# ScalarE instead of GpSimd makes the high halves of the weights in the index stage of a two-layer encoder

## The chip, the cores and the metric

The kernel runs on one core of one Trainium2 chip. The metric is the device time of one execution in microseconds (us). Engines are named as in the profile: PE is TensorE, ACT is ScalarE, DVE is VectorE, POOL is GpSimd, SP is SyncE; ACTq and SPq are the DMA issues of these engines.

## The reference

Two layers over 1024 tokens of width 1024. Layer 0 is attention of two kinds and a gated feed-forward. Layer 1 is sparse attention: an indexer scores all visible keys for each query, each query keeps its 256 best keys, and 16 heads attend to them. The change lies in the indexer:

```
h = x @ w_in
q, k_r, c_lat, q_idx, k_idx, w_idx = jnp.split(h, [c0, c1, c2, c3, c4], axis=-1)
q_idx = partial_rope(q_idx.reshape(b, s, IDX_HEADS, IDX_DIM), positions)   # 16 heads of 64
k_idx = partial_rope(k_idx, positions)
idx_logits = relu(einsum('bqhd,bsd->bhqs', q_idx, k_idx))
score = einsum('bqh,bqhs->bqs', w_idx, idx_logits) * IDX_SCALE
top_val, top_idx = lax.top_k(where(visible, score, -inf), 256)
```

All of it is float32. The kernel multiplies in bf16 by splitting every operand in two: a high half (the value rounded to bf16) and a low half (the value minus the high half, again bf16). A product is then three bf16 matmuls: high by high, high by low, low by high.

## The kernel before

Each engine has a program of its own, written out by hand, and runs it in that order; semaphores join them. Nothing reorders it.

**Weights.** SP loads strips of weights, 128 x 1024 float32 each, into four slots `w_stage[0..3]`. Each is split into `w_hi[slot]` and `w_lo[slot]`. SP may load a slot again when its low half is written (`w_split`). In the index stage of before both halves are made by POOL in `split_piece` (L266: multiply by one, write bf16; L269: subtract). Elsewhere a pair of helpers does it with two engines: `piece_hi` (L275) is an ACT copy, `piece_lo` (L282) the POOL subtraction.

**The index stage** follows the feed-forward of layer 0. Its sync, gpsimd, tensor, scalar and vector programs are `index_sync`, `index_gpsimd`, `index_tensor`, `index_scalar`, `index_vector`. Eight strips s = 0 to 7 of `l1_qidx` hold two index heads each, strip s in slot s % 4, so each slot is used twice (i = 0, then i = 1). While strip s is projected, POOL prepares the strip that comes four later: for s < 4 the second round of index strips, for s >= 4 the first four strips of `l1_q`, the query weights of the stage behind.

For each strip:

1. PE makes the projection in eight parts of six matmuls (L2012, `strip_unit`) into two PSUM banks. Between the parts it puts the score products of the strip two earlier (L2056, `scores(g)`).
2. ACT copies the strip to `strip_f` (L2084) and issues four DMAs (L2089) that bring it, with halves swapped, into `strip_w`. This is `copy_strip`.
3. DVE multiplies the PSUM copy by the cosine table (L2140). POOL multiplies `strip_w` by the sine table when the DMAs have landed (L2030, "the sine" below). DVE adds the two (L2146, "the rotation").
4. ACT rounds the rotated strip to bf16 (L2120, two instructions, `highs`), DVE makes the low half (L2178, `lows`).

**The scores.** A strip gives 12 score products, g = 12(s-2)+t with t = 0 to 11: two heads by six query blocks that see 384, 512, 640, 768, 896 and 1024 keys. For each, PE writes one of two PSUM bank pairs in turn (`bank = 2 * (g % 2)`), ACT applies ReLU into `positive[g % 4]` (L2112), and DVE multiplies by the head's weight and adds it to `score` (L2168, L2171, "the add"). PE waits before product g until ReLU g-2 is done (`pe.wait_ge(s_ir, g - 1)`), ACT before ReLU g until add g-4 is done.

ACT's order for one strip is `copy_strip`, ReLU t = 0 to 4, `highs`, ReLU t = 5 to 11, then the `copy_strip` of the next strip. DVE's is cosine, adds t = 0 to 2, rotation, adds t = 3 to 6, `lows`, adds t = 7 to 11. POOL's is the sine, then the split. Score products exist for ACT and DVE from s = 1 on.

At the stage's end PE waits for the last add (`pe.wait_ge(s_ia, IDX_STEPS * KT)`) before it goes on with the remaining query strips (L309), and DVE begins the search for the best 256 then.

Of the kernel before, what the change touches and what calls it, by code (L numbers as in the profile page):

```python
# [28 lines left out]
KT = D_MODEL // P  # L29
# [25 lines left out]
SLOTS = 4  # L55
# [48 lines left out]
def wait_if(eng, semaphore, value):  # L104

    if not isinstance(value, int) or value > 0:
        eng.wait_ge(semaphore, value)
# [39 lines left out]
def program(nc, t_in, out):  # L147
    with ExitStack() as ctx:
# [20 lines left out]
        def sem(name):  # L169
            return nc.alloc_semaphore(name)  # L170
# [30 lines left out]
        def banks(b):  # L201

            return ps[:, b:b + 2, :].rearrange("p a n -> p (a n)")


        w_loaded = [sem(f"w_loaded{s}") for s in range(SLOTS)]
        w_cast = [sem(f"w_cast{s}") for s in range(SLOTS)]
        w_split = [sem(f"w_split{s}") for s in range(SLOTS)]
        w_used = [sem(f"w_used{s}") for s in range(SLOTS)]
# [6 lines left out]
        def strips(name, per_body, iters):  # L216
            return Feed(uses, used, lambda n, i: t_in[name][per_body * i + n],
                        [(n, KT * P) for n in range(per_body)], iters)

        def row_tiles(name, tiles):  # L220

            return Feed(uses, used, lambda n, i: t_in[name][n % tiles],
                        [(n % SLOTS, D_MODEL) for n in range(2 * tiles)], 1)

        feed_o0 = row_tiles("l0_o", KT)
# [5 lines left out]
        feed_qidx = strips("l1_qidx", 4, 2)  # L231
        feed_q = strips("l1_q", 4, 8)
# [25 lines left out]
        def split_piece(pool, feed, n, i):  # L258
            slot, cols = feed.pieces[n]
            pool.wait_ge(w_loaded[slot], 16 * (feed.use(n, i) + 1))  # L260
            hi, lo = held(feed, n)
            if feed is feed_o0 and n >= SLOTS:
                pool.wait_ge(s_pj, 6 * N_PAIRS)
            else:
                pool.wait_ge(w_used[slot], feed.used(n, i))
            pool.tensor_tensor(hi, w_stage[slot][:, 0:cols], ones[:, 0:1].to_broadcast([P, cols]),  # L266
                               ALU.mult).then_inc(w_cast[slot], 1)
            pool.wait_ge(w_cast[slot], feed.use(n, i) + 1)
            pool.tensor_tensor(lo, w_stage[slot][:, 0:cols], hi, ALU.subtract).then_inc(w_split[slot], 1)  # L269

        def piece_hi(act, feed, n):
            slot, cols = feed.pieces[n]
            act.wait_ge(w_loaded[slot], 16 * (feed.use(n, 0) + 1))
            act.wait_ge(w_used[slot], feed.used(n, 0) - (feed is feed_o0 and n < KT + SLOTS))
            act.activation(w_hi[slot][:, 0:cols], w_stage[slot][:, 0:cols], ACT.Copy).then_inc(w_cast[slot], 1)  # L275

        def piece_lo(pool, feed, n):
            slot, cols = feed.pieces[n]
            pool.wait_ge(w_loaded[slot], 16 * (feed.use(n, 0) + 1))
            pool.wait_ge(w_used[slot], feed.used(n, 0) - (feed is feed_o0 and n < KT + SLOTS))  # L280
            pool.wait_ge(w_cast[slot], feed.use(n, 0) + 1)
            pool.tensor_tensor(w_lo[slot][:, 0:cols], w_stage[slot][:, 0:cols], w_hi[slot][:, 0:cols],  # L282
                               ALU.subtract).then_inc(w_split[slot], 1)

# [29 lines left out]
        def held(feed, n):  # L314

            if feed is feed_o0 and SLOTS <= n < KT:
                return xt_hi[:, n - SLOTS, :], xt_lo[:, n - SLOTS, :]
            slot, cols = feed.pieces[n]
            return w_hi[slot][:, 0:cols], w_lo[slot][:, 0:cols]
# [963 lines left out]
        def back_and_norm(tag, feed, tiles, act_hi, act_lo, names, free_at, bank_of, next_feed, early, load_x=None,  # L1283
# [161 lines left out]
            def scalar_program(act):  # L1445
# [18 lines left out]
                def piece_highs(first, last):  # L1464
                    if tiles == KT:
                        for n in range(first, last):
                            piece_hi(act, feed, n)
# [16 lines left out]
                if tiles == KT:  # L1484
                    piece_hi(act, next_feed, 0)
# [501 lines left out]
        def idx_step(g):  # L1987

            s, t = g // IDX_STEPS, g % IDX_STEPS
            return s, t // len(picky), picky[t % len(picky)], 2 * (g % 2)  # L1990

        def strip_bank(s):
            return 4 + 2 * (s % 2)
# [5 lines left out]
        def swaps_through(s):  # L1999


            return (64 if s % 2 == 0 else 32) + 64 * (s // 2 + 1)
# [24 lines left out]
        def index_gpsimd(pool):  # L2027
            def sine(w, tab, b, swapped):
                pool.wait_ge(s_sw5[b], swapped)
                pool.tensor_tensor(w, w, tab, ALU.mult).then_inc(s_s5, 1)  # L2030

            split_piece(pool, feed_qidx, 0, 0)
            pool.wait_ge(s_tl5, 64)
            sine(strip_w[0][:, :], rope_i[1][:, :], 0, 64)
            split_piece(pool, feed_qidx, 1, 0)
            sine(strip_w[1][0:ROPE, :], rope_q[1][:, :], 1, 32)
            split_piece(pool, feed_qidx, 2, 0)
            split_piece(pool, feed_qidx, 3, 0)
            for s in range(KT):
                sine(strip_w[s % 2][:, :], rope_i[1][:, :], s % 2, swaps_through(s))  # L2040
                if s < 4:
                    split_piece(pool, feed_qidx, s, 1)
                else:
                    split_piece(pool, feed_q, s - 4, 0)

        def index_tensor(pe):
            def scores(g):
# [31 lines left out]
        def index_scalar(act):  # L2079
            def copy_strip(m, bank, b, heads, used, swapped, rotated):  # L2080

                act.wait_ge(*used)
                wait_if(act, s_sw5[b], swapped)
                act.activation(strip_f[b][:, :], banks(bank), ACT.Copy).then_inc(s_f5, 1)  # L2084
                act.wait_ge(s_f5, m + 1)
                wait_if(act, s_a5, rotated)
                for a in range(0, 64 * heads, 32):
                    to = a + 32 if a % 64 == 0 else a - 32
                    act.dma_start(strip_w[b][to:to + 32, :], strip_f[b][a:a + 32, :]).then_inc(s_sw5[b], 16)  # L2089

            def small_used(n):
                return w_used[feed_small.slot(n)], feed_small.used(n, 0) + 1

            copy_strip(0, 0, 0, 2, small_used(0), 0, 0)
            copy_strip(1, 2, 1, 1, small_used(1), 0, 0)
            act.wait_ge(*small_used(2))
            act.activation(lat_hi[:, 1, :], banks(4), ACT.Copy).then_inc(s_h5, 1)
            act.wait_ge(*small_used(3))
            for h in range(2):
                src = ps[:, 6 + h, 0:4 * IDX_HEADS].rearrange("p (b n) -> p b n", b=4)  # L2100
                act.activation(w_idx[:, 4 * h:4 * h + 4, :], src, ACT.Copy, scale=IDX_SCALE).then_inc(s_w5, 1)
            act.wait_ge(s_a5, 1)
            act.activation(ki_hi[:, :], banks(0), ACT.Copy).then_inc(s_h5, 1)
            act.wait_ge(s_a5, 2)
            act.activation(lat_hi[:, 0, :], banks(2), ACT.Copy).then_inc(s_h5, 1)

            def relu(g):
                s, hh, i, bank = idx_step(g)
                act.wait_ge(s_iq, g + 1)
                if g >= 4:  # L2110
                    act.wait_ge(s_ia, g - 3)
                act.activation(positive[g % 4][:, 0:span[i]], banks(bank)[:, 0:span[i]], ACT.Relu).then_inc(s_ir, 1)  # L2112

            def highs(s):
                act.wait_ge(s_a5, 2 + s + 1)
                if s >= 2:
                    act.wait_ge(s_iq, IDX_STEPS * (s - 1))
                for hh in range(2):
                    rows = slice(hh * IDX_DIM, (hh + 1) * IDX_DIM)
                    act.activation(qi[s % 2][hh][rows, :], banks(strip_bank(s))[rows, :], ACT.Copy).then_inc(s_h5, 1)  # L2120

            for s in range(KT):
                copy_strip(2 + s, strip_bank(s), s % 2, 2,
                           (w_used[feed_qidx.slot(s % 4)], feed_qidx.used(s % 4, s // 4) + 1),
                           swaps_through(s) - 64, s + 1)
                for t in range(IDX_STEPS):
                    if s >= 1 and t < 5:
                        relu(IDX_STEPS * (s - 1) + t)
                    if t == 4:
                        highs(s)  # L2130
                    if s >= 1 and t >= 5:
                        relu(IDX_STEPS * (s - 1) + t)
            for t in range(IDX_STEPS):
                relu(IDX_STEPS * (KT - 1) + t)
# [612 lines left out]
```

## Time and profile before

| what | value |
|---|---|
| median of 3 runs | 2836.85 us (2831.59 to 2836.87) |
| profiled execution, its time | 2837.71 us |
| profiled execution, its span | 2835.9 us |
| PE busy | 2704.4 us (95%) |
| DVE busy | 1897.8 us (67%) |
| POOL busy | 1667.6 us (59%) |
| ACT busy | 1088.9 us (38%) |
| index stage, first strip to the first matmul behind it | 1286.98 to 1467.84 us of the span |

Busy time of PE includes the filling of its pipeline, so 95% is not a peak rate. The shares are means over the whole span; within the index stage they are others, and the engines there feed each other in a ring, so that a busy share alone does not say who sets the pace.

### The profile page before, as it was taken

The page shows a single profiled execution, that of the slowest core. Times are in us where ns is not written, and L with a number is a line of the kernel's source. Part 1 is how long each engine was busy: PE and PEld are TensorE (multiplying, and loading weights), DVE is VectorE, ACT ScalarE, POOL GpSimd, SP SyncE. Part 2 cuts the span into 40 slices and gives each one's busy share as a digit, 9 for nine tenths or more (in the row PEclk, how much of TensorE's full clock was granted, in tenths as well). Part 3 has the DMA queues.
Part 4 walks back from the last instruction along what each step waited for, and adds up shares of the span by engine and source line. Part 5 has one row for each costly group of instructions (what it writes and reads, how often), then busy time and mean ns, then how long its engine had stood idle before and what let it go on. Part 6 is the DMA issues. An engine that isn't in the chain of part 4 may idle for free.

```text
span 2835.9 us, 42627 instructions
## 1 busy us (share of the span) xinstructions
PE 2704.4 (95%) x16048; PEld 1358.3 (48%) x16048; DVE 1897.8 (67%) x2637; ACT 1088.9 (38%) x1665; POOL 1667.6 (59%) x916
## 2 busy tenths in 40 slices
PE   8999898899999999999899999889999999999998
PEld 4566554354444444444444444455554444444443
DVE  6787778576666674255999999777747756664043
ACT  3555556343333310014554343667743433331000
POOL 4676656336666779845347777711113566775884
PEclk9999999999999999999999999999999999999999
DMA  4222466631111253333213222588874211113332
GB/s 149 54 60 70 82 120 123 190 118 53 54 60 60 67 175 129 98 134 86 52 38 141 111 78 100 122 183 193 192 213 142 70 60 60 56 56 127 126 103 98
DMA packets 312621, 297.97 MB, mean 105 GB/s; under 512 B 252720, under 2 KB 252848, under 8 KB 312480
## 3 DMA queue, kind: packets, MB, share of 16 engines
q1 hardware_dynamic: 284832, 264.97, 32.4%
q10 hardware_dynamic: 27648, 31.07, 3.8%
q8 instruction: 94, 1.54, 0.2%
q14 instruction: 47, 0.39, 0.0%
HBM read 189.51 MB, written 35.70 MB: 79 GB/s over the span
## 4 chain that ended last, share of the span: by engine, by line
PE 79%; DVE 6%; DMA 5%; issue 4%; ACT 3%; POOL 2%; ACTq 1%; POOLq 0%; DVEq 0%; SPq 0%
PE ps L1684 23%; PE ps L327 20%; PE ps L309 14%; DMA pt<-split 5%; PE ps L643 4%; PE ps L2501 4%; PE ps L392 4%; PE ps L913 2%; PE ps L2012 2%; PE ps L2056 1%; PE ps L649 1%; DVE split L841 1%; PE ps L2518 1%; PE ps L884 1%; DVE prob L1037 1%
## 5 line engine op out<-in xcount | busy, mean ns | idle before, releaser
L266 POOL TENSOR_TENSOR w_hi<-w_stage,ones 128x1024 bf16<-128x1024 f32 (+1 forms) x115 | 238.3, 2072 | 137.7 <-PE ps L327 85.3
L269 POOL TENSOR_TENSOR w_lo<-w_stage,w_hi 128x1024 bf16<-128x1024 f32 (+1 forms) x115 | 266.0, 2313 | 9.0
L1501 DVE SCALAR_TENSOR_TENSOR x_res<-x_res,ps 128x1024 f32<-128x1024 f32 x32 | 39.0, 1218 | 319.7 <-PE ps L327 318.8
L327 PE MATMUL ps<-w_hi,hid_hi 128*128 128x512 bf16 x704 | 209.4, 379 | 0.8 <-POOL w_lo L269 0.8
L327 PE MATMUL ps<-w_hi,hid_lo 128*128 128x512 bf16 x704 | 209.4, 379 | 0.0
L327 PE MATMUL ps<-w_lo,hid_hi 128*128 128x512 bf16 x704 | 209.3, 379 | 0.0
L2501 PE MATMUL ps<-lat_hi,q_now 128*128 128x512 bf16 (+3 forms) x768 | 199.7, 330 | 6.7 <-DVE row_max L2566 6.7
L309 PE MATMUL ps<-xt_hi,w_hi 128*128 128x512 bf16 x608 | 181.5, 380 | 2.5 <-DVE score L2171 2.5
L309 PE MATMUL ps<-xt_hi,w_lo 128*128 128x512 bf16 x608 | 181.5, 380 | 0.0
L309 PE MATMUL ps<-xt_lo,w_hi 128*128 128x512 bf16 x608 | 181.3, 380 | 0.0
L1684 PE MATMUL ps<-xt_hi,w_hi 128*128 128x512 bf16 x432 | 163.7, 379 | 0.0
L1684 PE MATMUL ps<-xt_lo,w_hi 128*128 128x512 bf16 x432 | 163.7, 379 | 0.0
L1684 PE MATMUL ps<-xt_hi,w_lo 128*128 128x512 bf16 x432 | 163.7, 379 | 0.0
L1058 POOL TENSOR_TENSOR prob<-take,prob 128x1024 f32<-128x1024 f32 (+3 forms) x64 | 107.1, 1679 | 88.5 <-DVE prob L1037 70.5
L282 POOL TENSOR_TENSOR w_lo<-w_stage,w_hi 128x1024 bf16<-128x1024 f32 x28 | 66.1, 2367 | 149.4 <-ACT w_hi L275 149.4
L1449 ACT ACTIVATE ln_rstd<-ln_rstd 128x1 f32<-128x1 f32 x32 | 6.3, 202 | 374.6 <-DVE ln_rstd L1513 374.2
L2407 DVE MATCH_REPLACE8 score<-best,score 128x512 f32<-128x512 f32 (+4 forms) x160 | 148.8, 942 | 0.0
L1650 POOL TENSOR_TENSOR w_lo<-w_stage,w_hi 128x1024 bf16<-128x1024 f32 x36 | 76.9, 2136 | 113.6 <-ACT w_hi L1758 113.6
L2404 DVE MAX8 best<-score 128x8 f32<-128x512 f32 (+4 forms) x160 | 140.5, 944 | 1.8
L2624 POOL COPY v_now_hi<-val_hi 128x512 bf16 (+1 forms) x16 | 10.6, 661 | 217.9 <-PE ps L2518 217.8
L2566 DVE CUSTOM_DVE_ANT_0 prob<-ps,hide 128x1024 f32<-128x1024 f32 (+7 forms) x128 | 96.2, 751 | 59.9 <-PE ps L2501 59.8
L2550 ACT ACTIVATE prob<-prob,neg_max 128x1024 f32<-128x1024 f32 (+7 forms) x128 | 98.7, 771 | 70.4 <-DVE neg_max L2570 69.4
(305 smaller groups left out, 7581.2 us busy)
## 6 DMA issues: line engine op xcount, KB each, us to landing
w_stage<-in_l_up SPq DMA_DIRECT2D x88, 512.0 KB, 3.8
w_stage<-in_l_down SPq DMA_DIRECT2D x88, 512.0 KB, 3.7
w_stage<-in_l_o SPq DMA_DIRECT2D x32, 512.0 KB, 5.8
w_stage<-in_l_q SPq DMA_DIRECT2D x32, 512.0 KB, 5.2
q_split<-q_out SPq DMA_DIRECT2D x32, 512.0 KB, 2.6
q_now<-q_split SPq DMA_DIRECT2D x16, 1024.0 KB, 5.4
w_stage<-in_l_qkv SPq DMA_DIRECT2D x24, 512.0 KB, 4.1
x_spilled<-x_res ACTq DMA_DIRECT2D x16, 512.0 KB, 2.6
```

Of the source, the lines that this page charges most:

```text
L266: pool.tensor_tensor(hi, w_stage[slot][:, 0:cols], ones[:, 0:1].to_broadcast([P, cols]), ALU.mult).then_inc(w_cast[slot], 1)
L269: pool.tensor_tensor(lo, w_stage[slot][:, 0:cols], hi, ALU.subtract).then_inc(w_split[slot], 1)
L309: mm = pe.matmul(ps[:, bank + h, :], w, a[:, k, h * HALF:(h + 1) * HALF], start=(first and k == k0 and m == 0), stop=(last and k == k1 - 1 ...
L327: mm = pe.matmul(ps[:, bank + h, :], a[:, k, rows], w[:, h * HALF:(h + 1) * HALF], start=(k == first and m == 0), stop=(k == tiles - 1 and ...
L392: mm = pe.matmul(ps[:, bank + h, cols], w, a[:, k, h * HALF + cols.start:h * HALF + cols.stop], start=(k == 0 and m == 0), stop=(k == KT - ...
L643: mm = pe.matmul(ps[:, bank, :], w, a[:, u, h * HALF:(h + 1) * HALF], start=(u == 0 and m == 0), stop=(u == KT - 1 and m == 2))
L1058: pool.tensor_tensor(prob[t % 4][:, 0:n], take[t % 4][:, 0:n], prob[t % 4][:, 0:n], ALU.mult).then_inc(s_wsb, 1)
L1684: mm = pe.matmul(ps[:, bank, :], wk[:, k * P:(k + 1) * P], ak[:, k, :], start=(k == 0 and q == 0), stop=(k == 3 and q == 2))
L2404: dve.max(best[:, c, :], cells[c]).then_inc(s_top, 1)
L2407: dve.match_replace(cells[c], best[:, c, :], cells[c], TAKEN_SCORE).then_inc(s_rep, 1)
L2501: mm = pe.matmul(ps[:, 2 * (t % 2) + c // 512, 0:w], a, b, start=(kt == 0 and m == 0), stop=(kt == 1 and m == 2))
L2550: act.activation(prob7[t % 4][:, 0:n], prob7[t % 4][:, 0:n], ACT.Exp, scale=DSA_SCALE, bias=neg_max[:, t % 4:t % 4 + 1], accum_out=sum7[:, ...
```

## The change

In the index stage the 12 calls of `split_piece` on POOL become 12 calls of `piece_lo`, and ACT gets 12 calls of `piece_hi`: four at the start of its program, between the copies of the small projections, and one in each of the eight strips, between `copy_strip` and the first ReLU. Both helpers get the round i as an argument.

```diff
-        def piece_hi(act, feed, n):
+        def piece_hi(act, feed, n, i=0):
             slot, cols = feed.pieces[n]
-            act.wait_ge(w_loaded[slot], 16 * (feed.use(n, 0) + 1))
-            act.wait_ge(w_used[slot], feed.used(n, 0) - (feed is feed_o0 and n < KT + SLOTS))
+            act.wait_ge(w_loaded[slot], 16 * (feed.use(n, i) + 1))
+            act.wait_ge(w_used[slot], feed.used(n, i) - (feed is feed_o0 and n < KT + SLOTS))
             act.activation(w_hi[slot][:, 0:cols], w_stage[slot][:, 0:cols], ACT.Copy).then_inc(w_cast[slot], 1)
...
-            split_piece(pool, feed_qidx, 0, 0)
+            piece_lo(pool, feed_qidx, 0, 0)
             pool.wait_ge(s_tl5, 64)
             sine(strip_w[0][:, :], rope_i[1][:, :], 0, 64)
-            split_piece(pool, feed_qidx, 1, 0)
+            piece_lo(pool, feed_qidx, 1, 0)
             sine(strip_w[1][0:ROPE, :], rope_q[1][:, :], 1, 32)
-            split_piece(pool, feed_qidx, 2, 0)
-            split_piece(pool, feed_qidx, 3, 0)
+            piece_lo(pool, feed_qidx, 2, 0)
+            piece_lo(pool, feed_qidx, 3, 0)
             for s in range(KT):
                 sine(strip_w[s % 2][:, :], rope_i[1][:, :], s % 2, swaps_through(s))
                 if s < 4:
-                    split_piece(pool, feed_qidx, s, 1)
+                    piece_lo(pool, feed_qidx, s, 1)
                 else:
-                    split_piece(pool, feed_q, s - 4, 0)
+                    piece_lo(pool, feed_q, s - 4, 0)
...
             copy_strip(0, 0, 0, 2, small_used(0), 0, 0)
+            piece_hi(act, feed_qidx, 0)
             copy_strip(1, 2, 1, 1, small_used(1), 0, 0)
+            piece_hi(act, feed_qidx, 1)
             act.wait_ge(*small_used(2))
             act.activation(lat_hi[:, 1, :], banks(4), ACT.Copy).then_inc(s_h5, 1)
+            piece_hi(act, feed_qidx, 2)
             act.wait_ge(*small_used(3))
...
+            piece_hi(act, feed_qidx, 3)
...
                            swaps_through(s) - 64, s + 1)
+                if s < 4:
+                    piece_hi(act, feed_qidx, s, 1)
+                else:
+                    piece_hi(act, feed_q, s - 4, 0)
                 for t in range(IDX_STEPS):
```

ACT in strip s = 2, from the copy of the strip on, before the change (`positive` are the ReLUs, `qi` the highs; the numbers behind names are buffers):

```order
L2084 ACTIVATE strip_f_176<-ps 128x1024
L2089 DMA strip_w_178<-strip_f_176 32x1024 x4
L2112 ACTIVATE positive_180<-ps 128x384
L2112 ACTIVATE positive_181<-ps 128x512
L2112 ACTIVATE positive_182<-ps 128x640
L2112 ACTIVATE positive_183<-ps 128x768
L2112 ACTIVATE positive_180<-ps 128x896
L2120 ACTIVATE qi_170<-ps 64x1024
```

And the same place of the changed kernel:

```order
L2084 ACTIVATE strip_f_176<-ps 128x1024
L2089 DMA strip_w_178<-strip_f_176 32x1024 x4
L275 ACTIVATE w_hi_68<-w_stage_64 128x1024
L2116 ACTIVATE positive_180<-ps 128x384
L2116 ACTIVATE positive_181<-ps 128x512
L2116 ACTIVATE positive_182<-ps 128x640
L2116 ACTIVATE positive_183<-ps 128x768
L2116 ACTIVATE positive_180<-ps 128x896
L2124 ACTIVATE qi_170<-ps 64x1024
```

One row more stands between the four DMAs and the first ReLU; the ReLUs and highs keep their order.

POOL over strips s = 2 and s = 3 before the change (`strip_w` rows are the sines):

```order
L2030 TENSOR_TENSOR strip_w_178<-strip_w_178,rope_i_sin 128x1024
L266 TENSOR_TENSOR w_hi_68<-w_stage_64,ones 128x1024
L269 TENSOR_TENSOR w_lo_72<-w_stage_64,w_hi_68 128x1024
L2030 TENSOR_TENSOR strip_w_179<-strip_w_179,rope_i_sin 128x1024
L266 TENSOR_TENSOR w_hi_69<-w_stage_65,ones 128x1024
L269 TENSOR_TENSOR w_lo_73<-w_stage_65,w_hi_69 128x1024
```

And in the changed kernel:

```order
L2030 TENSOR_TENSOR strip_w_178<-strip_w_178,rope_i_sin 128x1024
L282 TENSOR_TENSOR w_lo_72<-w_stage_64,w_hi_68 128x1024
L2030 TENSOR_TENSOR strip_w_179<-strip_w_179,rope_i_sin 128x1024
L282 TENSOR_TENSOR w_lo_73<-w_stage_65,w_hi_69 128x1024
```

The low half now stands right behind the sine.

## Rows read from the trace of the kernel before

**Rows 1.** Page, chain that ended last, by engine, whole span.

```profile
PE 79%; DVE 6%; DMA 5%; issue 4%; ACT 3%; POOL 2%; ACTq 1%; POOLq 0%; DVEq 0%; SPq 0%
```

**Rows 2.** Stretch: us; busy PE, PEld, DVE, ACT, POOL; PE clock; DMA share, GB/s.

```profile
1360.00:1400.00 40.00, 36.01 (x179) 16.65 (x178) 39.30 (x33) 23.52 (x32) 15.29 (x7) 1.00 0.21 53
```

**Rows 3.** Waits of PE, 1225 to 1480 us: us in total, times, longest.

```profile
PE ps L2056 <- ACT positive L2112: 12.7, 13, 1.8
```

**Rows 4.** Timeline of ACT, strip s = 3: start, us, what [idle before, releaser].

```profile
1349.55 1.02 ACT L2084 ACTIVATE strip_f<-ps 128x1024 f32<-128x1024 f32 x1
1350.60 2.45 ACTq L2089 DMA_DIRECT2D strip_w<-strip_f  x4
1353.14 0.98 ACT L2112 ACTIVATE positive<-ps 128x384 f32<-128x384 f32 x2 [2.58 <-DVE score L2171]
...
1358.44 0.92 ACT L2112 ACTIVATE positive<-ps 128x896 f32<-128x896 f32 x1 [1.24 <-PE ps L2056]
1359.25 2.05 ACT L2120 ACTIVATE qi<-ps 64x1024 bf16<-64x1024 f32 x2
1361.33 1.41 ACT L2112 ACTIVATE positive<-ps 128x1024 f32<-128x1024 f32 x2
...
1369.38 1.02 ACT L2084 ACTIVATE strip_f<-ps 128x1024 f32<-128x1024 f32 x1
```

**Rows 5.** Timeline of PE, same strip, its two waits.

```profile
1353.69 0.39 PE L2056 MATMUL ps<-ki_hi,qi 128*128 128x512 bf16 x1 [1.77 <-ACT positive L2112]
1362.40 0.39 PE L2056 MATMUL ps<-ki_hi,qi 128*128 128x512 bf16 x1 [0.22 <-ACT positive L2112]
```

**Rows 6.** Timeline of DVE, same strip.

```profile
1353.69 0.61 DVE L2171 SCALAR_TENSOR_TENSOR score<-positive,w_idx,score 128x384 f32<-128x384 f32 x1
1354.22 0.75 DVE L2171 SCALAR_TENSOR_TENSOR score<-positive,w_idx,score 128x512 f32<-128x512 f32 x1
1355.18 2.67 DVE L2171 SCALAR_TENSOR_TENSOR score<-positive,w_idx,score 128x640 f32<-128x640 f32 x1 [0.22 <-ACT positive L2112]
1357.77 1.22 DVE L2146 TENSOR_TENSOR ps<-ps,strip_w 128x1024 f32<-128x1024 f32 x1
1358.91 1.51 DVE L2171 SCALAR_TENSOR_TENSOR score<-positive,w_idx,score 128x768 f32<-128x768 f32 x1
1360.34 4.21 DVE L2171 SCALAR_TENSOR_TENSOR score<-positive,w_idx,score 128x896 f32<-128x896 f32 x2
1363.27 1.80 DVE L2171 SCALAR_TENSOR_TENSOR score<-positive,w_idx,score 128x1024 f32<-128x1024 f32 x2
```

**Rows 7.** Timeline of POOL, strip s = 3, and one low half elsewhere.

```profile
1354.82 2.35 POOL L2030 TENSOR_TENSOR strip_w<-strip_w,rope_i_sin 128x1024 f32<-128x1024 f32 x1 [12.24 <-DMA strip_w<-strip_f]
1357.13 2.47 POOL L266 TENSOR_TENSOR w_hi<-w_stage,ones 128x1024 bf16<-128x1024 f32 x1
1359.68 2.72 POOL L269 TENSOR_TENSOR w_lo<-w_stage,w_hi 128x1024 bf16<-128x1024 f32 x1
...
1307.13 2.12 POOL L269 TENSOR_TENSOR w_lo<-w_stage,w_hi 128x1024 bf16<-128x1024 f32 x1
```

**Rows 8.** Timeline of ACT, a high half in the stage behind.

```profile
1493.43 1.04 ACT L2307 ACTIVATE w_hi<-w_stage 128x1024 bf16<-128x1024 f32 x1
1494.38 1.00 ACT L2317 ACTIVATE qs_f<-ps 128x1024 f32<-128x1024 f32 x1
```

**Rows 9.** Timeline of ACT in s = 0 and of PE in s = 1, waits.

```profile
1306.57 1.02 ACT L2120 ACTIVATE qi<-ps 64x1024 bf16<-64x1024 f32 x1 [7.99 <-DVE ps L2146]
1322.74 0.39 PE L2056 MATMUL ps<-ki_hi,qi 128*128 128x512 bf16 x1 [0.76 <-ACT positive L2112]
```

**Rows 10.** Behind the stage: timeline of PE, stretch, chain that ended last.

```profile
1467.84 0.60 PE L309 MATMUL ps<-xt_hi,w_hi 128*128 128x512 bf16 x2 [2.53 <-DVE score L2171]
1470.00:1472.00 2.00, 2.00 (x6) 0.73 (x5) 2.00 (x3) 0.00 (x0) 2.00 (x2) 0.50 0.00 0
1467.84 12.22 PE ps L309 x48
```

More of the change, by code:

```diff
@@ L269, in split_piece, with piece_lo @@
             pool.tensor_tensor(lo, w_stage[slot][:, 0:cols], hi, ALU.subtract).then_inc(w_split[slot], 1)
-        def piece_hi(act, feed, n):
+        def piece_hi(act, feed, n, i=0):
             slot, cols = feed.pieces[n]
-            act.wait_ge(w_loaded[slot], 16 * (feed.use(n, 0) + 1))
-            act.wait_ge(w_used[slot], feed.used(n, 0) - (feed is feed_o0 and n < KT + SLOTS))
+            act.wait_ge(w_loaded[slot], 16 * (feed.use(n, i) + 1))
+            act.wait_ge(w_used[slot], feed.used(n, i) - (feed is feed_o0 and n < KT + SLOTS))
             act.activation(w_hi[slot][:, 0:cols], w_stage[slot][:, 0:cols], ACT.Copy).then_inc(w_cast[slot], 1)
-        def piece_lo(pool, feed, n):
+        def piece_lo(pool, feed, n, i=0):
             slot, cols = feed.pieces[n]
-            pool.wait_ge(w_loaded[slot], 16 * (feed.use(n, 0) + 1))
-            pool.wait_ge(w_used[slot], feed.used(n, 0) - (feed is feed_o0 and n < KT + SLOTS))
-            pool.wait_ge(w_cast[slot], feed.use(n, 0) + 1)
+            pool.wait_ge(w_loaded[slot], 16 * (feed.use(n, i) + 1))
+            pool.wait_ge(w_used[slot], feed.used(n, i) - (feed is feed_o0 and n < KT + SLOTS))
+            pool.wait_ge(w_cast[slot], feed.use(n, i) + 1)
             pool.tensor_tensor(w_lo[slot][:, 0:cols], w_stage[slot][:, 0:cols], w_hi[slot][:, 0:cols],
```

## The prediction

> **What bounds the kernel now.** I read the chain that ended last first: 79% of it is PE [rows 1], so time counts where it holds PE up. Next the stretches of the index stage. In a steady one of 40 us DVE is busy for 39.30, PE for 36.01, ACT for 23.52 and POOL for 15.29 [rows 2]. That looks like a stage bound by DVE; a busy share, though, also holds the time in which an instruction stands blocked. So I read the waits of PE: it waits for ACT's ReLU, 13 times, 12.7 us in all [rows 3]. Then the timelines of the four engines over one strip.
>
> The strips repeat every 19.83 us: the copies of strips 3 and 4 start at 1349.55 and 1369.38 [rows 4]. I count from the copy, C = 0. ACT: copy to 1.02, four DMA issues to 3.50, first ReLU at 3.59, fifth at 8.89, the two highs at 9.70, sixth ReLU at 11.78, to 12.80 (its instruction takes 1.02 as the copy of the same width does) [rows 4]. PE waits twice: 1.77 us for the first ReLU, until 4.14, and 0.22 us for the sixth, until 12.85 [rows 5]. From 12.85 to the next copy at 19.83 PE runs its products and ACT follows, 6.98 us. So the pace is a ring: copy, DMA issues, first ReLU, PE, fifth ReLU, highs, sixth ReLU, PE, next copy. DVE stands in it only by the rotation, which the highs need.
>
> DVE looks full because POOL blocks it. The add of 640 keys issues at 1355.18, takes 2.67 us and ends 0.68 us behind POOL's sine, which ran from 1354.82 to 1357.17 [rows 6, 7]. The rotation, which has one input in PSUM, takes 1.22 us beside POOL's next instruction, unhindered [rows 6, 7]. Then the two engines take turns: the add of 768 ends late (1.51 us), POOL's low half takes 2.72 us where alone it takes 2.12, and the add of 896, issued at 1360.34, has not released the engine before 1363.27, 0.87 us behind the low half's end at 1362.40 [rows 6, 7]. That last pair is what matters here: the low half had been issued (1359.68) while the add of 768 ran, the add of 896 came directly behind that add, and POOL went first.
>
> **The change, part by part.** *Removed from POOL:* 12 instructions, 2.47 us each in the strip shown [rows 7]. POOL idles 12.24 us before its sine [rows 7], so its own time is worth nothing; worth something is only what it blocks.
>
> *Added to ACT:* 12 copies of 128 x 1024. The same operation takes 1.04 us, and the next instruction starts 0.95 us behind it [rows 8]; I take 0.95. Bounds of its price on the path: 0 where ACT is idle, 1.04 where it is not.
>
> The four at the start and the one in s = 0 fall into idle time: in s = 0 ACT idles 7.99 us before its highs [rows 9]. The sine of the first strip comes somewhat later, but the DVE rotation it feeds waits behind another DVE instruction anyway. In s = 1 PE waits 0.76 us for the sixth ReLU, which hangs on the sine's DMAs, issued ahead of the new copy [rows 9]; that hides the few tenths the first ReLU passes on. I cost both at 0; without this cover s = 1 would cost 0.95.
>
> In s = 2 to 7, six strips, the copy lies between DMA issues and first ReLU, on the ring. First ReLU: 3.59 + 0.95 = 4.54. PE waits 1.77 + 0.95 = 2.72 us there. Were that all, each strip would cost 0.95, together 5.7 us.
>
> *Moved by it:* the turns between DVE and POOL. The sine hangs on the DMAs, which stand ahead of the new copy, so it is still issued at 1354.82 - 1349.55 = 5.27. The first add (384) moves from 4.14 to 5.09 and gives way to the next after 0.53 (1353.69 to 1354.22), at 5.62 [rows 6]. So the sine is now issued *inside* the first add, where in the trace it came inside the second. By the turn that the low half and the add of 896 show, POOL is next:
> - sine from 5.62; it takes 2.35, less the 0.05 of its start-up: ends 7.92;
> - the add of 512 was held; it gives way 0.60 behind the sine by the 640 row (1357.77 against 1357.17), less about 0.13 for 128 keys fewer (384 and 512 rows: 0.61 and 0.75): 8.39;
> - the low half was issued at 7.9, since no high half stands between now; it is waiting when this add ends, goes ahead of the add of 640 and ends 2.06 behind it (1362.40 against 1360.34): 10.45;
> - the add of 640 gives way 0.60 later: 11.05; the rotation takes 1.22: 12.27, where it ended at 9.44;
> - highs at 12.31 instead of 9.70 + 0.95 = 10.65; sixth ReLU 2.08 later at 14.39, done at 15.41; PE goes on at 15.46 instead of 12.85.
>
> From there 6.98 us to the next copy: 22.44 against 19.83, 2.61 a strip, and six strips make 15.7 us. Of this 5.7 is the copy's own and 10.0 the rotation's delay. The relief of DVE behind the low half buys nothing, since the adds are not on the ring; only the rotation is.
>
> The Trainium skill ("SBUF — State Buffer", "Who interferes with whom") says that a VectorE instruction with two SBUF inputs and a GpSimd instruction that reads SBUF exclude each other for a whole instruction, the first to issue winning, and one with at most one SBUF input does not contend. By that rule the sum is the same 15.7, and the rule speaks against a change that shifts adds into a POOL instruction. The trace agrees in the rows named, 2.67 against 1.22 us.
>
> *PE's clock.* Behind a wait of 2.53 us PE's granted clock fell to half, 1.2 instead of 2.4 GHz, and 48 matmuls took 12.22 us [rows 10]; at the pace of a steady stage (pairs 0.43 us apart) they take 10.4. One fall so costs 1.8 us of PE time. The waits of 1.77 us did not bring it down: clock 1.00 [rows 2, 5]. The new first wait, 2.72 us, probably does in some strips. But PE then has 15.46 - 12.85 - 0.95 + 0.22 = 1.88 us of waiting ahead of it at the sixth ReLU, which takes up nearly all. I add 0.5, between 0 and 6 x 1.8 = 10.8, near 0 because of that cover. By the rule of thumb on idle gaps in the Trainium skill ("TensorE: Matmul & The Clock Gate", "HAM oscillation") gaps as short as this leave the clock alone, and the addition would be 0; the fall behind 2.53 us contradicts it.
>
> Behind the stage DVE and PE both start on the last add, so the delay is passed on whole. Sum: 15.7 + 0.5 = 16.2. Against the profiled execution's 2837.71 that is 2853.9; the median of the runs shown, 2836.85, lies 0.9 below, so 2853.
>
> **The rivals.**
> *Only ACT's 0.95 counts.* If the second add gets ahead of the sine (the DMAs land 0.35 us later than I reckon) or the low half comes too late to take its turn, the rotation is done before the highs are due at 10.65 and a strip costs 0.95: 5.7 us. Here PE has no cover for a fallen clock, so up to three falls add 0 to 5: 2842.5 to 2848. For it: 0.35 us is little. Against: the sine's issue lies inside the first add by 0.18 us at one end and 0.35 at the other.
>
> *Nothing to measure.* ACT's wait ahead of the first ReLU is booked as a wait for DVE's score (2.58 us) [rows 4]. Were the DMA issues no work of ACT's and this a true wait, the copy would hide in it: 0 to 4 us, 2837 to 2841. Against: issues fill that wait to within 0.09 us.
>
> *Faster.* DVE, at 39.30 of 40 us, is the bound after all. Without the high half the low half is done beside the rotation; the add of 768 waits 0.2 us more, and that of 896 is not held: 2.93 us to the next start (1360.34 to 1363.27) [rows 6] become about 1.06, by 0.13 for each 128 keys above the 0.53 of 384. That is 1.6 us a strip, seven strips, 11 us: 2826. It decides this way if the first ReLU has 0.95 us to spare. Against: DVE's wait of 0.22 us, right behind that ReLU [rows 6], and PE's of 1.77 show that it has none.
>
> **How the numbers follow.** Forecast 0.60 (its own range 2849 to 2857: 0.85 to 1.05 for the copy, falls of the clock), ACT's own price alone 0.22, nothing 0.10, faster 0.08. The range leaves the last two out, but for their edge: 2841 to 2857. 0.2% is 5.7 us, about what a measurement of this kernel can tell from no change. Faster 0.08; within 0.2% the third case and a fifth of the second, 0.15; slower 0.77.
>
> **What would show it.** Right: copies of strips 3 to 7 lie 22.4 us apart; the add of 512 takes about 2.8 us and the add of 640 about 2.7, instead of 0.75 and 2.67; the sine takes 2.65 us instead of 2.35; PE waits 2.7 us for the first ReLU and near 1.9 for the sixth; DVE's busy time in 40 us falls. The copies of the high halves take 1.04 us. If strips lie 20.8 apart and only the add of 640 is long, the first rival holds; if 19.8 or less, one of the others. Wrong it would be made by other turns between DVE and POOL than the one row shows, and by a clock that falls also between the sixth ReLU and the next copy, where nothing covers it.

## The result and the profile after

| | before | changed |
|---|---|---|
| median | 2836.83 us (2831.59 to 2836.87, 5 runs) | 2853.11 us (2848.22 to 2855.99, 5 runs) |
| profiled execution, span | 2835.9 us | 2854.2 us |

The ratio is 1.006, 95% interval 1.0046 to 1.0074: 16.3 us slower, where 16.2 were forecast.

The waits of PE in the index stage of the changed kernel:

```profile
PE ps L2056 <- ACT positive L2116: 23.3, 13, 2.9
```

The stretch of it that answers to [rows 2]:

```profile
1360.00:1400.00 40.00, 35.00 (x166) 16.08 (x168) 35.64 (x30) 22.56 (x28) 8.62 (x4) 0.97 0.14 40
```

PE waits as often as in [rows 3], 13 times, but 23.3 us instead of 12.7. DVE's busy time has fallen from 39.30 to 35.64 us of 40 and POOL's from 15.29 to 8.62. But these 40 us hold fewer strips. Over exactly one strip, s = 3, before and then after the change:

```profile
1349.55:1369.38 19.83, 17.84 (x90) 8.24 (x89) 19.49 (x17) 11.61 (x16) 7.50 (x3) 1.00 0.20 53
1353.07:1375.54 22.47, 19.43 (x88) 8.65 (x89) 19.39 (x17) 12.54 (x18) 5.15 (x2) 0.92 0.17 47
```

POOL was relieved (7.50 to 5.15 us a strip); DVE, the engine that looked full, was not (19.49 to 19.39): the time that it lost in the adds of 640 and 896 keys it now loses in those of 512 and 640, as the rows below show.

The timeline of ACT over strip s = 3 of the changed kernel, against [rows 4]:

```profile
1353.07 1.02 ACT L2084 ACTIVATE strip_f<-ps 128x1024 f32<-128x1024 f32 x1
1354.12 2.46 ACTq L2089 DMA_DIRECT2D strip_w<-strip_f  x4
1356.68 1.06 ACT L275 ACTIVATE w_hi<-w_stage 128x1024 bf16<-128x1024 f32 x1 [2.59 <-issue]
1357.64 0.96 ACT L2116 ACTIVATE positive<-ps 128x384 f32<-128x384 f32 x2
...
1365.42 2.05 ACT L2124 ACTIVATE qi<-ps 64x1024 bf16<-64x1024 f32 x2
1367.49 1.41 ACT L2116 ACTIVATE positive<-ps 128x1024 f32<-128x1024 f32 x2
...
1375.54 1.02 ACT L2084 ACTIVATE strip_f<-ps 128x1024 f32<-128x1024 f32 x1
```

From copy to copy 22.47 us, where it was 19.83. The first ReLU starts 4.57 us behind the strip's copy (forecast 4.54), the highs 12.35 behind it (12.31), the sixth ReLU 14.42 (14.39). DVE and POOL over the same strip, against [rows 6] and [rows 7]:

```profile
1358.15 0.62 DVE L2179 SCALAR_TENSOR_TENSOR score<-positive,w_idx,score 128x384 f32<-128x384 f32 x1 [1.71 <-ACT positive L2116]
1358.68 2.84 DVE L2179 SCALAR_TENSOR_TENSOR score<-positive,w_idx,score 128x512 f32<-128x512 f32 x1
1361.44 2.74 DVE L2179 SCALAR_TENSOR_TENSOR score<-positive,w_idx,score 128x640 f32<-128x640 f32 x1
1364.11 1.22 DVE L2154 TENSOR_TENSOR ps<-ps,strip_w 128x1024 f32<-128x1024 f32 x1
```

```profile
1358.35 2.62 POOL L2030 TENSOR_TENSOR strip_w<-strip_w,rope_i_sin 128x1024 f32<-128x1024 f32 x1 [17.27 <-DMA strip_w<-strip_f]
1360.93 2.58 POOL L282 TENSOR_TENSOR w_lo<-w_stage,w_hi 128x1024 bf16<-128x1024 f32 x1
```

The sine is issued at 1358.35, while the add of 384 runs (1358.15 to 1358.77). The add of 512 now takes 2.84 us instead of 0.75: it stands behind the sine. The low half, issued at 1360.93, goes next, and the add of 640 stands behind it for 2.74 us. The rotation starts 11.04 us behind the copy, where it started at 8.22. PE's two waits of the strip, against [rows 5]:

```profile
1358.17 0.39 PE L2056 MATMUL ps<-ki_hi,qi 128*128 128x512 bf16 x1 [2.71 <-ACT positive L2116]
1368.57 0.39 PE L2056 MATMUL ps<-ki_hi,qi 128*128 128x512 bf16 x1 [0.22 <-ACT positive L2116]
```

The second is 0.22 us, not the 1.9 forecast. In strips 2, 4 and 6 it is as forecast; this is the one of strip 4:

```profile
1390.98 0.39 PE L2056 MATMUL ps<-ki_hi,qi 128*128 128x512 bf16 x1 [1.87 <-ACT positive L2116]
```

The clock explains the difference. Stretches of the changed kernel, in strips 1, 3, 5 and 7, and one of strip 4:

```profile
1311.00:1314.00 3.00, 2.97 (x8) 1.15 (x8) 0.56 (x2) 1.44 (x2) 0.26 (x1) 0.51 0.65 148
1359.00:1362.00 3.00, 3.00 (x8) 1.03 (x7) 3.00 (x2) 0.63 (x1) 3.00 (x2) 0.50 0.00 0
1404.00:1406.00 2.00, 2.00 (x7) 0.68 (x5) 2.00 (x1) 0.70 (x1) 2.00 (x2) 0.50 0.00 0
1448.00:1450.00 2.00, 2.00 (x7) 0.85 (x8) 2.00 (x2) 1.04 (x2) 1.91 (x1) 0.50 0.00 0
1380.00:1383.00 3.00, 2.38 (x13) 1.20 (x14) 2.40 (x2) 1.76 (x4) 2.16 (x1) 1.00 0.10 21
```

Behind the first wait (2.69 to 2.94 us) the granted clock stood at half, 1.2 GHz, in strips 3, 5 and 7, and not in strips 2, 4 and 6; in strip 1 it fell behind a wait of 2.25 us ahead of PE's projection of strip 2. Where it fell in strips 3, 5 and 7, PE's slow matmuls filled the time in which it would have waited for the sixth ReLU, and the strip is no longer for it: strips 2 to 6 last 22.42, 22.47, 22.41, 22.44 and 22.42 us.

### The profile page after: what moved, and what is told of

Its sections match the earlier page's. It is cut to its first block, busy times and chain, and to the rows that moved or that the text cites. A ratio compares the mean times of both kernels' runs of the same rounds, so it can differ in the third digit from the quotient of the medians.

```text
span 2854.2 us, 42372 instructions
## 1 busy us (share of the span) xinstructions
PE 2698.2 (95%) x15781; PEld 1362.2 (48%) x16048; DVE 1895.6 (66%) x2637; ACT 1100.4 (39%) x1677; POOL 1641.3 (58%) x904
## 4 chain that ended last, share of the span: by engine, by line
PE 77%; DVE 8%; issue 5%; DMA 4%; ACT 4%; POOL 2%; ACTq 1%; DVEq 0%; POOLq 0%; SPq 0%
PE ps L1684 23%; PE ps L327 19%; PE ps L309 13%; PE ps L643 4%; PE ps L2509 4%; PE ps L392 3%; DMA pt<-split 3%; PE ps L913 2%; PE ps L2012 1%; PE ps L649 1%; PE ps L2056 1%; DVE split L841 1%; PE ps L884 1%; DVE split L2568 1%; PE ps L2526 1%
## 5 line engine op out<-in xcount | busy, mean ns | idle before, releaser
L266 POOL TENSOR_TENSOR w_hi<-w_stage,ones 128x1024 bf16<-128x1024 f32 (+1 forms) x103 | 211.9, 2057 | 116.8 <-PE ps L327 85.3
L269 POOL TENSOR_TENSOR w_lo<-w_stage,w_hi 128x1024 bf16<-128x1024 f32 (+1 forms) x103 | 236.7, 2298 | 8.1
L282 POOL TENSOR_TENSOR w_lo<-w_stage,w_hi 128x1024 bf16<-128x1024 f32 x40 | 94.3, 2363 | 177.8 <-ACT w_hi L275 177.8
L2509 PE MATMUL ps<-lat_hi,q_now 128*128 128x512 bf16 (+3 forms) x737 | 188.1, 328 | 6.3 <-DVE row_max L2574 6.3
L309 PE MATMUL ps<-xt_hi,w_hi 128*128 128x512 bf16 x598 | 179.1, 380 | 3.1 <-DVE score L2179 2.5
L309 PE MATMUL ps<-xt_hi,w_lo 128*128 128x512 bf16 x596 | 178.9, 380 | 0.8 <-issue 0.2
L1684 PE MATMUL ps<-xt_hi,w_hi 128*128 128x512 bf16 x422 | 159.9, 379 | 0.5
L1684 PE MATMUL ps<-xt_hi,w_lo 128*128 128x512 bf16 x422 | 159.9, 379 | 0.3
L1650 POOL TENSOR_TENSOR w_lo<-w_stage,w_hi 128x1024 bf16<-128x1024 f32 x36 | 76.9, 2135 | 114.0 <-ACT w_hi L1758 114.0
L2509 PE MATMUL ps<-lat_lo,q_now 128*128 128x512 bf16 (+3 forms) x384 | 124.7, 329 | 3.1 <-issue 1.0
```

The lines of the kernel that those rows point to most:

```text
L309: mm = pe.matmul(ps[:, bank + h, :], w, a[:, k, h * HALF:(h + 1) * HALF], start=(first and k == k0 and m == 0), stop=(last and k == k1 - 1 ...
L1684: mm = pe.matmul(ps[:, bank, :], wk[:, k * P:(k + 1) * P], ak[:, k, :], start=(k == 0 and q == 0), stop=(k == 3 and q == 2))
L2509: mm = pe.matmul(ps[:, 2 * (t % 2) + c // 512, 0:w], a, b, start=(kt == 0 and m == 0), stop=(kt == 1 and m == 2))
```

## The experiments

Each kernel was timed with the kernel before on the same chip; its median there was 2835.29 us for the first four (31 runs) and 2835.23 for the others (33 runs).

**The sine moved back into the second add** (`e1_turn`).

```diff
+                if s >= 2:
+                    pool.wait_ge(s_ia, IDX_STEPS * (s - 1) + 1)
                 sine(strip_w[s % 2][:, :], rope_i[1][:, :], s % 2, swaps_through(s))
```

> The changed kernel, with one wait more: in strips 2 to 7 POOL issues the sine only when the first add (384 keys) is done, so that it comes inside the second add (512 keys), as it did before the change. A wait is added, nothing is taken away. If the turns between DVE and POOL make up 10 of the 16 us: strips 20.8 us apart instead of 22.4, PE's first wait 2.7 us, the add of 512 back at 0.75 us, the add of 640 long, and 5.7 us above the kernel before plus 0 to 5 for falls of PE's clock that nothing covers now: 2842.5 to 2848. If instead the high half on ACT costs 2.6 us a strip by itself (the rival), the wait changes nothing or adds to it: strips 22.4 us or more, 2853 or more.

Measured: 2841.68 us (12 runs), ratio 1.0027 (1.0019 to 1.0036). One wait more leaves the change 6.4 us above the kernel before instead of 16.3. DVE and POOL in strip s = 3, and the copies of strips 3, 4, 5 and 6:

```profile
1357.43 0.75 DVE L2181 SCALAR_TENSOR_TENSOR score<-positive,w_idx,score 128x512 f32<-128x512 f32 x1
1358.40 2.66 DVE L2181 SCALAR_TENSOR_TENSOR score<-positive,w_idx,score 128x640 f32<-128x640 f32 x1 [0.23 <-ACT positive L2118]
1360.99 1.22 DVE L2156 TENSOR_TENSOR ps<-ps,strip_w 128x1024 f32<-128x1024 f32 x1
...
1357.59 2.80 POOL L2030 TENSOR_TENSOR strip_w<-strip_w,rope_i_sin 128x1024 f32<-128x1024 f32 x1 [17.00 <-DVE score L2181]
...
1351.83 1.02 ACT L2086 ACTIVATE strip_f<-ps 128x1024 f32<-128x1024 f32 x1
1372.59 1.02 ACT L2086 ACTIVATE strip_f<-ps 128x1024 f32<-128x1024 f32 x1
1393.36 1.02 ACT L2086 ACTIVATE strip_f<-ps 128x1024 f32<-128x1024 f32 x1
1415.82 1.02 ACT L2086 ACTIVATE strip_f<-ps 128x1024 f32<-128x1024 f32 x1
```

The add of 512 is back at 0.75 us, and the strips are 20.76 and 20.77 us apart, but for two. Strip 5 is 22.46: there the clock fell behind the 2.70 us wait (granted 0.50 in the stretch from 1400 to 1402). Strip 2 is 22.47, with the same fall behind a wait of 2.93 us (granted 0.50 from 1335 to 1338). With no later wait to hide it a fall costs 1.70 us. So the same fall is free in the changed kernel and dear here.

**The low half held behind the rotation** (`e2_lo_late`).

```diff
                 sine(strip_w[s % 2][:, :], rope_i[1][:, :], s % 2, swaps_through(s))
+                if s >= 2:
+                    pool.wait_ge(s_a5, 2 + s + 1)
```

> The changed kernel, with the low half of strips 2 to 7 held until the rotation of the strip is done. The sine still comes inside the first add and holds the add of 512 keys, but no low half can go ahead of the add of 640. If the low half's turn is what makes the rotation late: rotation done 10.4 us behind the strip's copy instead of 12.3, before the highs are due at 10.65; strips 20.8 us apart, 2842.5 to 2848, as with the sine moved. If the sine's turn alone is enough to make it late: strips 22.4 us, 2853. The low half now runs beside the adds of 768 and 896 keys, which then take long without any cost.

Measured: 2840.64 us (11 runs), ratio 1.0022 (1.0013 to 1.0031). Strips 3 to 6 are each 20.77 us long. DVE and POOL in strip s = 3, whose copy is at 1350.57:

```profile
1356.17 2.84 DVE L2181 SCALAR_TENSOR_TENSOR score<-positive,w_idx,score 128x512 f32<-128x512 f32 x1
1358.93 0.87 DVE L2181 SCALAR_TENSOR_TENSOR score<-positive,w_idx,score 128x640 f32<-128x640 f32 x1
1359.73 1.22 DVE L2156 TENSOR_TENSOR ps<-ps,strip_w 128x1024 f32<-128x1024 f32 x1
...
1355.85 2.61 POOL L2030 TENSOR_TENSOR strip_w<-strip_w,rope_i_sin 128x1024 f32<-128x1024 f32 x1 [12.77 <-DMA strip_w<-strip_f]
1361.03 2.82 POOL L282 TENSOR_TENSOR w_lo<-w_stage,w_hi 128x1024 bf16<-128x1024 f32 x1 [2.57 <-DVE ps L2156]
```

The sine still holds the add of 512, for 2.84 us, but the add of 640 takes 0.87 and the rotation ends 10.38 us behind the copy, in time for the highs. Both turns are needed for the loss; either one taken away gives back the same 1.65 us a strip. The clock fell here too, in strips 1 and 7. Both medians lie just under the times expected (2842.5 to 2848); as differences to the kernel before on the same chip they are 6.4 and 5.4 us, against 5.7 for the copy's own price.

**The high half behind the highs** (`e3_after_highs`), in strips 2 to 7.

```diff
                     if t == 4:
                         highs(s)
+                        if s >= 2:
+                            high_half()
```

(`high_half` here and below is the call of `piece_hi` that stood behind `copy_strip`.)

> The changed kernel, with the high half of strips 2 to 7 moved from behind the DMA issues to behind the highs, just ahead of the sixth ReLU. It is still on the ring, but behind the rotation, and the first add, the sine and the second add lie as before the change. ACT's own price by itself: PE's first wait 1.77 us as before, its second 0.22 + 0.95 = 1.17 us, strips 20.8 us apart, 5.7 us above the kernel before, 2842.5; no wait of PE is long enough to bring its clock down, so nothing is added. If the price of 2.6 us a strip hung on the copy itself and not on where it stands, 2852.

Measured: 2844.21 us (7 runs), ratio 1.0028 (1.0017 to 1.0039). ACT in strip s = 3 around the copy, and PE's two waits:

```profile
1360.06 2.05 ACT L2124 ACTIVATE qi<-ps 64x1024 bf16<-64x1024 f32 x2
1362.13 1.06 ACT L275 ACTIVATE w_hi<-w_stage 128x1024 bf16<-128x1024 f32 x1
1363.21 1.02 ACT L2116 ACTIVATE positive<-ps 128x1024 f32<-128x1024 f32 x1
...
1354.49 0.39 PE L2056 MATMUL ps<-ki_hi,qi 128*128 128x512 bf16 x1 [1.88 <-ACT positive L2116]
1364.29 0.39 PE L2056 MATMUL ps<-ki_hi,qi 128*128 128x512 bf16 x1 [1.30 <-ACT positive L2116]
```

The mechanism held, the size was off: strips are 21.04 us apart (20.8 expected), because here the next ReLU starts 1.08 us behind the copy and not 0.95, and PE's waits are 1.30 and 1.88 us instead of 1.17 and 1.77. Price 1.2 us a strip. Strip 1, which this edit leaves as the change has it, is 1.15 us longer than before; its clock fell behind the wait ahead of strip 2, as in the changed kernel.

**The high half between the third and fourth ReLU** (`e4_hidden`), in strips 2 to 7.

```diff
+                    if s >= 2 and t == 3:
+                        high_half()
                     if s >= 1 and t < 5:
                         relu(IDX_STEPS * (s - 1) + t)
```

> The changed kernel, with the high half of strips 2 to 7 between the third and the fourth ReLU, where ACT idled 1.24 us for PE in every strip. The copy takes 0.95 us of that and is done before the sine ends, so the low half can start behind the sine. If the ring sets the pace: strips 19.8 us apart as before, DVE's busy share down by about 1.6 us a strip with nothing gained, 2837 (2834 to 2840). If DVE sets it (the rival that forecast faster): strips 18.2 to 19 us apart and 2826 to 2832.

Measured: 2837.40 us (11 runs), ratio 1.0002 (0.9993 to 1.0011): no difference that can be told. The timeline of ACT in strip s = 3:

```profile
1355.40 0.70 ACT L2116 ACTIVATE positive<-ps 128x640 f32<-128x640 f32 x1 [0.32 <-PE ps L2056]
1356.00 1.05 ACT L275 ACTIVATE w_hi<-w_stage 128x1024 bf16<-128x1024 f32 x1
1357.35 0.81 ACT L2116 ACTIVATE positive<-ps 128x768 f32<-128x768 f32 x1 [0.30 <-PE ps L2056]
```

The stretch of 40 us from 1355:

```profile
1355.00:1395.00 40.00, 35.83 (x177) 16.72 (x179) 36.44 (x34) 25.17 (x33) 10.05 (x4) 1.00 0.20 54
```

The copy fits into the wait for PE, which shrinks from 1.24 to 0.30 us. DVE has 36.44 busy us in 40 instead of 39.12 in the same stretch before, and the strips stay at 19.83 us; since their length is the same, DVE really is relieved here. That settles the rival in which DVE is the bound: relief alone is worth nothing.

**Only the first six high halves** (`e5_cover`): ACT makes those of the four first strips and of strips 0 and 1; in strips 2 to 7 POOL makes both halves.

```diff
                 sine(strip_w[s % 2][:, :], rope_i[1][:, :], s % 2, swaps_through(s))
-                if s < 4:
+                if s < 2:
                     piece_lo(pool, feed_qidx, s, 1)
+                elif s < 4:
+                    split_piece(pool, feed_qidx, s, 1)
                 else:
-                    piece_lo(pool, feed_q, s - 4, 0)
+                    split_piece(pool, feed_q, s - 4, 0)
...
-                if s < 4:
+                if s < 2:
                     piece_hi(act, feed_qidx, s, 1)
-                else:
-                    piece_hi(act, feed_q, s - 4, 0)
```

> One part of the change alone: ACT makes the high halves of the four first strips and of strips 0 and 1, six of twelve; in strips 2 to 7 POOL makes both halves as before the change. If idle time covers these six: 2837, strips 2 to 7 19.8 us apart and strip 1 at most 0.2 us longer than before, but for a fall of PE's clock behind the wait of 2.3 us ahead of strip 2, which depends on where the wait lies and can cost 1.1 us. If the first copies delay the stage by themselves: copies of the strips 1 us or more later than before from strip 0 on.

Measured: 2836.55 us (10 runs), ratio 1.0003 (0.9994 to 1.0013). Strips 2 to 6 are 19.83 to 19.87 us. Strip 1 is 21.62 us instead of 21.06, 0.56 more without any fall of the clock; I had given it 0.2 at most. Its adds show why (DVE, then POOL, strip s = 1, copy at 1308.97; the last row is the add of 512 before the change):

```profile
1314.66 2.29 DVE L2176 TENSOR_SCALAR score<-positive,w_idx 128x512 f32<-128x512 f32 x1 [0.20 <-ACT positive L2118]
1316.87 2.41 DVE L2176 TENSOR_SCALAR score<-positive,w_idx 128x640 f32<-128x640 f32 x1
...
1314.28 2.38 POOL L2030 TENSOR_TENSOR strip_w<-strip_w,rope_i_sin 128x1024 f32<-128x1024 f32 x1 [6.67 <-DMA strip_w<-strip_f]
...
1314.34 0.49 DVE L2168 TENSOR_SCALAR score<-positive,w_idx 128x512 f32<-128x512 f32 x1 [1.19 <-ACT positive L2112]
```

Before the change, SP issued the next load of slot 0 at 1309.28, together with the strip's own DMAs, and the sine of strip 1 was issued 7.22 us behind the copy. With the low half done earlier that load goes out at 1307.63, the DMAs land sooner and the sine comes at 5.31, on top of the adds: the same two turns once more. That the loads' time did it is read from the issue times, not tested.

**The DMAs issued by SP, nothing else** (`e6_sp_only`), and with SP's DMAs **the high half between the ReLUs** (`e7_sp_hidden`) or **the change as it stands** (`e8_sp_change`).

```diff
-                for a in range(0, 64 * heads, 32):
-                    to = a + 32 if a % 64 == 0 else a - 32
-                    act.dma_start(strip_w[b][to:to + 32, :], strip_f[b][a:a + 32, :]).then_inc(s_sw5[b], 16)
...
             load_first(sp, feed_qidx)
+            swap(0, 0, 2, 0)
+            swap(1, 1, 1, 0)
             load_rest(sp, feed_qidx)
-            load_first(sp, feed_q)
+            for s in range(KT):
+                swap(2 + s, s % 2, 2, s + 1)
+                if s < 4:
+                    load_piece(sp, feed_q, s, 0)
```

(`swap` holds the waits and the four issues that ACT had.)

> The kernel before, with nothing of the change, but the four DMAs of each strip are issued by SP instead of ACT. This takes 2.45 us of issuing out of the ring. If DVE, held up by POOL's three instructions a strip, is the next to set the pace: strips still 19.8 us apart, PE's wait for the first ReLU gone but its waits elsewhere longer, 2832 to 2838. If the ring is the only bound: strips 17.9 to 18.5 us apart, 2825 to 2829.

> DMAs issued by SP, and the high half of strips 2 to 7 on ACT between the third and fourth ReLU. Here the relief of DVE should be worth something, since the ring no longer hides it: strips 19.1 us apart (the rotation, behind the sine and the third add, becomes the bound), 0.75 us a strip or 4.5 us in all below the kernel before: 2830 to 2834. If the relief is worth nothing here either, the same as with the DMAs on SP alone. If the ring with its DMA issues was the only bound, both are at 2825 to 2829.

> The change as it stands, ACT's high half right behind the strip's copy, but the DMAs issued by SP. With 2.45 us of issues gone, the copy of 0.95 us no longer moves the first add onto the sine: the adds of 384 and 512 keys are done before the sine is issued. Strips 19.1 us apart, 2830 to 2834, 20 us below the change with the DMAs on ACT. If the copy's place costs 2.6 us a strip whatever stands ahead of it: strips 20 us or more apart.

| | strips | median | ratio |
|---|---|---|---|
| DMAs on SP, both halves on POOL | 19.83 us (strips 3 to 5) | 2836.84 (11 runs) | 1.0008 (0.9999 to 1.0017) |
| DMAs on SP, high half between ReLUs | 19.09 us (one 19.31) | 2829.01 (11 runs) | 0.9980 (0.9970 to 0.9989) |
| DMAs on SP, high half as in the change | 19.09 us | 2829.18 (11 runs) | 0.9979 (0.9970 to 0.9988) |

The stretch of 40 us from 1355 with only the DMAs moved to SP, and behind it the adds of 640 and 896 keys of the same kernel:

```profile
1355.00:1395.00 40.00, 35.80 (x180) 16.86 (x179) 39.75 (x34) 23.99 (x31) 15.26 (x7) 1.00 0.15 40
```

```profile
1355.27 2.97 DVE L2178 SCALAR_TENSOR_TENSOR score<-positive,w_idx,score 128x640 f32<-128x640 f32 x1
1360.73 3.01 DVE L2178 SCALAR_TENSOR_TENSOR score<-positive,w_idx,score 128x896 f32<-128x896 f32 x1
```

The same stretch with the DMAs on SP and the change as it stands:

```profile
1355.00:1395.00 40.00, 37.52 (x187) 17.39 (x186) 32.69 (x33) 26.13 (x33) 10.26 (x5) 1.00 0.16 40
```

With 2.45 us of issues out of ACT's part of the ring and POOL's work as it was, nothing is gained: DVE, 39.75 us of 40, sets the pace at the very length the ring had. (Strip 2 is shorter, 19.22 us, and strip 6 longer, 21.29: there the clock fell to 0.56, behind a wait of 2.15 us.) Only now is the relief worth something: with it DVE falls to 32.69, PE rises to 37.52 and a strip loses 0.74 us. With the change as it stands the sine is issued 5.23 us behind the copy, and no add stands behind it: the three first adds are done 0.11 us later. What holds the strip then is the sine itself: the rotation waits 2.35 us for it, and the highs 0.89 us for the rotation. The medians lie 6 us below the kernel before, 1 us under the range expected and 1.6 more than six strips account for; the clock was not followed run by run. The last kernel is faster than both that the study began with.

## Why the prediction was right

**The ring.** Its pace was read as copy, DMA issues, ReLUs, highs, PE, and DVE's full row as blocked time. Hiding the copy left the strips at 19.83 us with DVE relieved, and lengthening the ring lengthened them. One thing I did not see: DVE with POOL's three instructions, once the ring is shortened, needs the same 19.83 us. The ring and DVE were level, and the kernel could not be made faster by either alone.

**The copy's own price.** Forecast 0.95 us a strip; 20.77 less 19.83 is 0.94 where the turns were taken out, in two different ways. Behind the highs the same copy cost 1.21.

**The turns.** Forecast 10.0 us over six strips from one row, the add of 896. Strips 2 to 6 grew from 99.23 us together to 112.16 (copy of strip 2 to that of strip 7), 2.59 each for 2.61, and from the last copy to the end of the stage the time grew from 38.90 to 41.48. That is 15.5 for 15.7. The rule named from the Trainium skill ("SBUF — State Buffer", "Who interferes with whom"), by which the sum was the same, holds in this trace: the held adds, with two inputs in SBUF, take 2.84 and 2.74 us, and the rotation, with one, takes 1.22 beside POOL's low half (`e1_turn`, issued 1360.99, inside the low half from 1360.34 to 1363.05).

**DVE's relief.** Forecast as worth nothing, since the adds are not on the ring. `e4_hidden` shows that. The sign named for it, DVE's busy time in 40 us, is a poor one: it fell because the strips grew, and over one strip DVE was as busy as before.

**The rivals.** ACT's price alone came true in the two kernels in which a turn was removed (6.4 and 5.4 us above the kernel before); its two conditions, a sine at least 0.35 us later or a low half too late for its turn, are what the two added waits made. The rival in which DVE is the bound is settled by `e4_hidden`. The copy did not hide in the DMA issues: the row now books the same 2.6 us as issue.

**What was mis-sized.** The step "I cost both at 0" was wrong for strip 1. It cost 0.56 us by the turns, and in the profiled execution 1.15, since the clock fell there too (22.21 against 21.06 us). The 0.5 for the clock was not lost inside strips 2 to 7; the fall in strip 1 cost 0.6. Of the 18.3 us by which the span grew, 16.45 are spent by the end of the stage; the other 1.85 lie behind it, where this execution had a half-clock stretch that the one before had not (stretch of the changed kernel, then the corresponding one before). The same instruction of ACT comes 15.31 us later just ahead of that stretch (2107.08 against 2091.77), and another 18.27 us later behind it (2185.85 against 2167.58).

```profile
2110.00:2116.00 6.00, 5.12 (x32) 3.16 (x34) 0.33 (x1) 0.55 (x1) 0.00 (x0) 0.50 0.31 60
```

```profile
2091.00:2098.00 7.00, 4.63 (x81) 3.35 (x77) 2.84 (x12) 2.30 (x8) 0.00 (x0) 1.00 0.83 159
```

I take these 1.85 us for chance, since the runs of one kernel spread over 8 us, and the part behind the stage took 1362.6 us in `e1_turn`, 1368.1 before and 1369.9 in the changed kernel, though nothing differs there; no run separates them.

That the total came out at 16.3 us for 16.2 is in part luck: the 95% interval of the ratio stands for 13 to 21 us, strip 1 cost 1.15 that the sum had at 0, and the 0.5 for the clock in strips 2 to 7 was not spent. What is borne out is the price of strips 2 to 7.

## What to carry to other kernels

A busy row may hold blocked time: compare one operation's duration where it runs alone and where it overlaps GpSimd before calling VectorE the bound. When an instruction is added to an engine in a ring, ask not only what it costs there but which instructions elsewhere it shifts against each other; here 0.95 us became 2.6, one more wait took back 1.65 of it, and another place for the same copy all of it. Compare busy times over the same piece of work, here a strip, and not over the same number of microseconds. When a relief brings nothing, look for the second bound at the same height, and remove both together.

## What the runs showed of the hardware

- A GpSimd instruction issued while one VectorE add runs or stands blocked goes ahead of the VectorE add that follows directly: in each of strips 2 to 7 of the changed kernel (2.83 to 2.84 and 2.74 to 2.75 us for adds that take 0.75 and 0.87 alone). A `TENSOR_SCALAR` from SBUF to SBUF is held likewise (2.29 us in `e5_cover`, 0.49 before).
- A wait of 2.70 us brought TensorE's clock to 1.2 GHz in some strips and not in others of the same execution; a wait of 2.25 us ahead of strip 2 did so in the changed kernel (clock 0.51) and one of the same 2.25 us did not in `e1_turn` (1.00). The shortest wait that the clock fell behind in the stage was 2.15 us (0.56, `e6_sp_only`), and two others of 2.15 us in that execution left it at 1.00. What decides it was not tested. A fall cost 1.70 us in two strips of `e1_turn`, where no later wait took it up, and nothing where one did.
- A ScalarE copy of 128 partitions lets the next instruction start 0.95 to 0.96 us behind it; the same copy placed ahead of the 1024-key ReLU, behind the two of 64 partitions, took 1.08. What makes the difference was not tested.
